# Latent-attention scores from split operands, and one decay product per head, in a four-layer block on one Trainium2 core

## The reference, cut to what matters

```
qn_l, qr_l = queries(cq_l, seq)
q_l = jnp.concatenate([qn_l, apply_rope(qr_l, cos, sin)], axis=-1)
...
s = jnp.einsum('bqhd,bkhd->bhqk', q, k).astype(F32) * ((C_NOPE + C_ROPE) ** -0.5)
p = jax.nn.softmax(s, axis=-1)
```

```
s = jnp.einsum('bhqd,bhkd->bhqk', qc, kh).astype(jnp.float32) * scale
s = s + (cq[..., :, None] - csum[:, :, None, :])
s = jnp.where(kpos[None, :] <= qpos[:, None], s, -jnp.inf)
```

## Time and profile before

| | |
|---|---|
| time, median of 3 runs | 1072.35 us (1072.02 to 1072.69) |
| the profiled execution | 1071.89 us |
| its span, first to last instruction | 1069.9 us |
| PE busy | 1049.8 us (98%) |
| DVE busy | 733.3 us (69%) |
| ACT busy | 591.8 us (55%) |
| chain that ended last | PE 89%, DVE 7%, ACT 2% |
| DMA | 165.41 MB, mean 155 GB/s |

### The profile page before, as it was taken

How to read it: one execution, slowest core, us unless ns; L and a number is a source line. 1 busy time by engine, 2 the same in 40 slices (tenths; PEclk the granted TensorE clock), 3 DMA queues, 4 the chain that set the end, 5 groups by cost and what they waited for, 6 DMA issues and landing times.

```text
span 1069.9 us, 18034 instructions
## 1 busy us (share of the span) xinstructions
PE 1049.8 (98%) x6797; PEld 884.3 (83%) x6797; DVE 733.3 (69%) x1577; ACT 591.8 (55%) x1209; POOL 2.6 (0%) x10
## 2 busy tenths in 40 slices
PE   5999999999999999999999999999999999999997
PEld 3677776788997779989898988889988898888886
DVE  4635567665588756787778766658788778765665
ACT  4534245543364446568776764445567677665444
POOL 0000000000000000000000000000000000000000
PEclk9999999999999999999999999999999999999999
DMA  9998551222342224564555566666464545555662
GB/s 326 336 311 245 181 184 41 60 60 75 83 135 55 78 78 126 140 175 138 138 141 155 145 170 182 193 196 177 129 171 139 139 139 157 157 162 177 194 213 83
DMA packets 203551, 165.41 MB, mean 155 GB/s; under 512 B 7101, under 2 KB 172713, under 8 KB 203465
## 3 DMA queue, kind: packets, MB, share of 16 engines
q1 hardware_dynamic: 202944, 163.28, 52.0%
q0 software_dynamic: 192, 0.66, 0.2%
q10 hardware_dynamic: 328, 0.32, 0.1%
HBM read 163.18 MB, written 1.05 MB: 153 GB/s over the span
## 4 chain that ended last, share of the span: by engine, by line
PE 89%; DVE 7%; ACT 2%; issue 1%; DMA 1%; SPq 0%; ACTq 0%; DVEq 0%
PE pj L2059 23%; PE pj L2061 22%; PE pj L2060 22%; DVE w_lo L1328 2%; PE pj L2153 2%; PE tr L2611 1%; PE ac L2415 1%; PE ac L2550 1%; PE sc L2259 1%; PE tr L2266 1%; PE sc L2401 1%; ACT w_hi L835 1%; PE ac L2280 1%; PE sc L2532 1%; PE sc L2530 1%
## 5 line engine op out<-in xcount | busy, mean ns | idle before, releaser
L1328 DVE TENSOR_TENSOR w_lo<-raw,w_hi 128x1024 fp32r<-128x1024 f32 (+2 forms) x258 | 309.4, 1202 | 148.7 <-ACT w_hi L835 147.8
L835 ACT ACTIVATE w_hi<-raw 128x1024 fp32r<-128x1024 f32 (+2 forms) x258 | 268.0, 1040 | 89.3 <-PE pj L2061 87.3
L2059 PE MATMUL pj<-h_hi,w_hi 128*128 128x256 f32 (+1 forms) x960 | 299.0, 311 | 0.2
L2061 PE MATMUL pj<-h_hi,w_lo 128*128 128x256 f32 (+1 forms) x960 | 291.1, 303 | 0.0
L2060 PE MATMUL pj<-h_lo,w_hi 128*128 128x256 f32 (+1 forms) x960 | 291.0, 303 | 0.0
L2059 PEld LDWEIGHTS pj<-h_hi,w_hi 128*128 128x128 f32 x960 | 183.7, 191 | 19.1 <-issue 10.4
L2061 PEld LDWEIGHTS pj<-h_hi,w_lo 128*128 128x128 f32 x960 | 183.8, 191 | 7.4
L2060 PEld LDWEIGHTS pj<-h_lo,w_hi 128*128 128x128 f32 x960 | 184.0, 192 | 6.2
L2059 PE MATMUL pj<-w_hi,h_hi 128*128 128x512 f32 x344 | 137.4, 399 | 0.4 <-DVE h_lo L1402 0.4
L2061 PE MATMUL pj<-w_hi,h_lo 128*128 128x512 f32 x344 | 134.2, 390 | 0.0
L2060 PE MATMUL pj<-w_lo,h_hi 128*128 128x512 f32 x344 | 134.2, 390 | 0.0
(11 more groups left out here) (358 smaller groups left out, 1473.4 us busy)
## 6 DMA issues: line engine op xcount, KB each, us to landing
raw<-in_w_in_dram SPq DMA_DIRECT2D x152, 512.0 KB, 3.7
ada_raw<-in_ada_w_dram SPq DMA_DIRECT2D x48, 512.0 KB, 7.9
raw<-in_even_w_in_dram SPq DMA_DIRECT2D x28, 512.0 KB, 5.0
raw<-in_w_branch_dram SPq DMA_DIRECT2D x24, 512.0 KB, 3.7
raw<-in_w_out_dram SPq DMA_DIRECT2D x16, 512.0 KB, 3.7
raw<-in_odd_w_in_dram SPq DMA_DIRECT2D x11, 512.0 KB, 3.9
raw<-in_even_w_out_dram SPq DMA_DIRECT2D x8, 512.0 KB, 3.7
raw<-in_odd_w_out_dram SPq DMA_DIRECT2D x8, 512.0 KB, 3.8
```

The costliest lines, as they stand in the source:

```text
L835: last = nc.scalar.activation(hi, src, ACT.Copy)
L1328: last = nc.vector.tensor_tensor(lo, src, hi.bitcast(F32), ALU.subtract)
L2059: nc.tensor.matmul(dst, lh, rh, start=first, stop=False)
L2061: return nc.tensor.matmul(dst, ll, rh, start=False, stop=final)
```

## The change

Four things change.

1. The unrotated scores of the latent attention are made from split operands. `qn` and `kn` are written as a rounded copy by ACT (`qn_hi`, `kn_hi`) and a rest by DVE (`qn_lo`, `kn_lo`), the two in that order on the same bank, and DVE frees it. One `F32` product for a head and a query tile becomes three `F32R` products. The values `vm` are read out by ACT instead of DVE.
2. The decay rows are stored in three blocks of 128 columns, so that one product of 384 columns per head replaces two of 128 and 256.
3. At the start, `condition_turn(0)` and `condition(1)` stand before `spread(0, 4)`, `condition_turn(1)` before `turn_x(4)`, and ACT copies the third set of sums before `modulated_hi(0, 1)`.
4. The last norm takes one step of another form: a reciprocal, one combined operation, a reciprocal, in place of a reciprocal and three operations.

```
-        keys = [("kn", 4 * i + j, "dve" if 4 * i + j in DVE_KEYS else "act") for j in range(4)]
-        return keys + [("vm", (i, t), "dve") for t in range(4)]
+        return [("kn", 4 * i + j, "dve") for j in range(4)] + [("vm", (i, t), "act") for t in range(4)]
     if name == "wq":
-        return [("qn", 2 * i, "act"), ("qn", 2 * i + 1, "act"), ("qr", i, "act")]
+        return [("qn", 2 * i, "dve"), ("qn", 2 * i + 1, "dve"), ("qr", i, "act")]
...
-        decays = [h_hi[:, 0, EARLY[lay]] for lay in range(LAYERS_2)]
+        decays = [h_hi[:, 0:3, EARLY[lay].start:EARLY[lay].start + P] for lay in range(LAYERS_2)]
...
@@ ACT, l1_evacuate
                     elif kind == "kn":
-                        nc.scalar.activation(kn_o[:, i, :], src, ACT.Copy).then_inc(freed["act"], 1)
+                        nc.scalar.activation(kn_hi[:, i, :], src, ACT.Copy).then_inc(nope_hi, 1)
+                    elif kind == "vm":
+                        half, n = i
+                        nc.scalar.activation(v_o[:, n, 512 * half:512 * half + 512], src, ACT.Copy).then_inc(freed["act"], 1)
                     elif kind == "qn":
-                        nc.scalar.activation(qn_o[:, i, :], src[:, 0:SEQ], ACT.Copy, scale=MLA_SCALE).then_inc(freed["act"], 1)
+                        nc.scalar.activation(qn_hi[:, i, :], src[:, 0:SEQ], ACT.Copy, scale=MLA_SCALE).then_inc(nope_hi, 1)
...
@@ DVE, l1_evacuate
-                    elif kind == "vm":
-                        half, n = i
-                        proj_ready(dve, g, None)
-                        nc.vector.tensor_scalar(v_o[:, n, 512 * half:512 * half + 512], bank(g), 1.0, None, ALU.mult)\
+                    elif kind == "qn":
+                        dve.wait_ge(nope_hi, NOPE_ORDER.index((kind, i)) + 1)
+                        nc.vector.scalar_tensor_tensor(qn_lo[i], bank(g)[:, 0:SEQ], MLA_SCALE, qn_hi[:, i, :].bitcast(F32),
+                                                       ALU.mult, ALU.subtract).then_inc(freed["dve"], 1)
+                    elif kind == "kn":
+                        dve.wait_ge(nope_hi, NOPE_ORDER.index((kind, i)) + 1)
+                        nc.vector.tensor_tensor(kn_lo[i], bank(g).rearrange("p (a n) -> p a n", a=2),
+                                                kn_hi[:, i, :].bitcast(F32).rearrange("p (a n) -> p a n", a=2), ALU.subtract)\
                             .then_inc(freed["dve"], 1)
...
-                if s == WKV_SLOT[1]:
-                    for i in DVE_KEYS:
-                        keys_evacuate(i)
...
@@ DVE, the last norm
-                after(nc.vector.reciprocal(y, root))
-                newton(y, term, v).then_inc(last_set, 1)
+                after(nc.vector.reciprocal(term, root))
+                after(nc.vector.scalar_tensor_tensor(term, term, v, root, ALU.mult, ALU.add))
+                nc.vector.reciprocal(y, term).then_inc(last_set, 1)
...
@@ PE, the start
-            spread(0, 4)
             condition_turn(0)
             condition(1)
+            spread(0, 4)
+            condition_turn(1)
             turn_x(4)
-            condition_turn(1)
...
@@ PE, l1_scores
-                    nc.tensor.matmul(sc[:, e, :], qn_o[:, 2 * hp + e, q], kn_o[:, 2 * hp + e, :], start=True, stop=False)
+                    h = 2 * hp + e
+                    nc.tensor.matmul(sc[:, e, :], qn_hi[:, h, q], kn_hi[:, h, :], start=True, stop=False)
+                    nc.tensor.matmul(sc[:, e, :], qn_lo[h][:, q], kn_hi[:, h, :], start=False, stop=False)
+                    nc.tensor.matmul(sc[:, e, :].rearrange("p (a n) -> p a n", a=2), qn_hi[:, h, q], kn_lo[h], start=False,
+                                     stop=False)
...
@@ PE, pair_scores
-                            nc.tensor.matmul(sc[:, e, 0:128], one, decay[0:N_DECAY, 0:P], start=False, stop=False)
-                            last = nc.tensor.matmul(sc[:, e, 128:384], one, decay[0:N_DECAY, :], start=False, stop=True)
+                            last = nc.tensor.matmul(sc[:, e, 0:384].rearrange("p (b n) -> p b n", b=3), one,
+                                                    decay[0:N_DECAY, :, :], start=False, stop=True)
```

More of the change, by code:

```diff
@@ L210 @@
 LAST_OF_CHUNK2 = {c: g for g, (_, _, _, c) in enumerate(G2)}
+NOPE_ORDER = [(k, i) for k, i, _, _ in G1 if k in ("qn", "kn")]
 LAST_GROUP = [LAST_OF_CHUNK1.get(c, -1) for c in range(CB)]
@@ L432, in build_program @@
         w_hi, w_lo = sb("w_hi", [P, NSPLIT, WEL], F32R), sb("w_lo", [P, NSPLIT, WEL], F32R)
+        with nc.sbuf_tensor("parts_o", [P, 7680], F32R) as parts_o:
+            pass
         work = sb("work", [P, 12288])
@@ L478, in build_program @@
         kr_o = work[:, 0:512]
-        qn_o = work[:, 512:2560].rearrange("p (h n) -> p h n", h=C_HEADS)
+        qn_hi = parts_o[:, 512:2560].rearrange("p (h n) -> p h n", h=C_HEADS)
+        qn_lo = [w[:, 3072 + SEQ * h:3072 + SEQ * h + SEQ] for w in (m_hi, m_lo) for h in range(C_HEADS // 2)]
         qr_o = work[:, 2560:3584].rearrange("p (h n) -> p h n", h=4)
-        kn_o = work[:, 3584:7680].rearrange("p (h n) -> p h n", h=C_HEADS)
+        kn_hi = parts_o[:, 3584:7680].rearrange("p (h n) -> p h n", h=C_HEADS)
+        kn_lo = [w[:, 2 * h:2 * h + 2, CTX] for w in (h_hi, h_lo) for h in range(C_HEADS // 2)]
         v_o = work[:, 7680:11776].rearrange("p (n c) -> p n c", n=4)
@@ L579, in build_program @@
         recip_set = sem("recip_set")
+        nope_hi = sem("nope_hi")
         og_set, g_hi_set, g_lo_set = sem("og_set"), sem("g_hi_set"), sem("g_lo_set")
@@ L914, in _ @@
             x_turned_to(6)
+            ada_evacuate(2)
             modulated_hi(0, 1)
@@ L917, in _ @@
             for pair in range(1, 4):
-                ada_evacuate(2 * pair)
+                if pair > 1:
+                    ada_evacuate(2 * pair)
                 ada_evacuate(2 * pair + 1)
@@ L1075, in l1_evacuate @@
                     src = bank(g)
-                    if kind == "vm" or (kind == "kn" and engine == "dve"):
-                        continue
                     proj_ready(act, g, None)
@@ L1979, in _ @@
                         dve.wait_ge(tr_free, TB + lay * NT2 + TR2_OF[("cf", 0)] + 1)
[L1980 to L1985, removed]
-                                                decay[96:N_DECAY, :].bitcast(F32), ALU.subtract).then_inc(decay_set, 1)
+                        decay = decays[lay][:, 1:3, :]
+                        rest = decay_rest.rearrange("p (a n) -> p a n", a=2)
+                        after(nc.vector.tensor_scalar(decay[0:N_DECAY], rest[0:N_DECAY], 1.0, None, ALU.mult))
+                        after(nc.vector.tensor_tensor(rest[64:N_DECAY], rest[64:N_DECAY], decay[64:N_DECAY].bitcast(F32),
+                                                      ALU.subtract))
+                        after(nc.vector.tensor_scalar(decay[64:N_DECAY], rest[64:N_DECAY], 1.0, None, ALU.mult))
+                        after(nc.vector.tensor_tensor(decay[96:N_DECAY], rest[96:N_DECAY], decay[96:N_DECAY].bitcast(F32),
+                                                      ALU.subtract))
+                        nc.vector.tensor_scalar(decays[lay][0:N_DECAY, 0, :], decay[0:N_DECAY, 0, :].bitcast(F32), 1.0, None,
+                                                ALU.mult).then_inc(decay_set, 1)
                     if s == MISC_SLOT and lay + 1 < LAYERS_2:
@@ L2020, in last_gained @@
                 dve.wait_ge(y_sq, n + 1)
-                part = nc.vector.tensor_scalar(col[:, 1, 2 + n:3 + n], y_squares[:, n:n + 1], 1.0 / D, NORM_EPS, ALU.mult, ALU.add)
+                part = nc.vector.tensor_scalar(col[:, 1, 2 + n:3 + n], y_squares[:, n:n + 1], 0.25 / D, 0.25 * NORM_EPS, ALU.mult,
+                                               ALU.add)
                 after(part)
```

7 lines of the change are left out of this document (1 added, 6 removed).

## The result

| | before | changed |
|---|---|---|
| median | 1072.18 us (4 runs, 1071.45 to 1072.69) | 1077.76 us (4 runs, 1075.5 to 1078.54) |
| ratio, 95% interval | | 1.0054 (1.0039 to 1.007) |
| profiled execution | 1071.89 us | 1075.5 us |
| its span | 1069.9 us | 1073.6 us |
| mean granted clock, profiled execution | 0.997 | 0.996 |

The change made the kernel slower by 5.6 us. The profiled execution is the quickest of the four, only 3.6 above that of before, and its mean granted clock is higher than that of the other three.

The account below looks back on a forecast made before the run. PE, busy 98% of the span, was taken as the bound. Scores 3.6 us lost, less 1.5 decay, 0.2 start, 0.2 norm: 1.7 more, 1074.1; clock +0.8 −1.7 gave 1073.2, range 1069.0 to 1076.2.

Parts of the forecast that it names:

- A stall of 2.5 us: Before the first key group of wkv 0, PE waits for DVE's qn reading; pair 0's scores 3.3 us late together.
- The fourth key group of `wkv 1`: PE's group at wkv 1 waits for DVE's first key reading: 3.2 us late, pair 1's 0.42 gain used up.
- one new fall of the clock partly hidden, the old one gone: Likeliest case: stalls, a new half-clock stretch at +0.8 us, the one near 438 us saved at −1.7; 1073.2, chance 0.36.
- The third case: Stalls, old clock fall stays, a new one at wkv 1's fourth key group: 1074.9, or 1075.8 if unhidden; chance 0.30.
- The rule of the Trainium skill: For PE's two new waits: half clock after each, up to 3.4 us more in sum, by the advice against idle gaps.
- The products of the scores: Latent attention on PE: six F32R products cost 1.38 instead of 1.80 us, gaining 0.42 a pair, 3.4 over eight.
- The decay products: Decay product on PE: two of 384 columns take 0.34 instead of 0.56 us; 0.9 to 1.8 gained, 1.5 taken.
- The start: Start of the kernel: PE's 0.8 us wait for ACT goes, but later sums are tied to transfers; 0.2 gained.
- The norm: Last norm, at the chain's end: one DVE step fewer, 0.2 us gained.
- The fourth case: DVE reaches the banks sooner, no stalls: 1067.1, or 1070.8 if only the first goes; chance 0.20 for both.

Follow-up runs that it names:

- filled: Changed kernel plus 11 and 15 idle PE products ahead of the first key group of wkv 0 and the last of wkv 1; 1073.54 us, ratio 1.0021.
- after_again: The changed kernel run once more, unaltered, for another profiled execution; 1076.97 us, ratio 1.0054.
- keys_early: Changed kernel with new order in slots 10 to 12 alone: wkv 1 keys copied before pair 1's exponentials, read before its scaling; 1071.35 us, ratio 0.9997.
- both_early: Changed kernel with keys_early's order, and queries and keys of wkv 0 read before rotations and weight pieces; 1068.36 us, ratio 0.9968.
- early_act: both_early with ACT's copies of qn 0 and qn 1 moved ahead of the two weight pieces of slot 8; 1068.05 us, ratio 0.9967.
- split_early: Kernel before with the split scores alone, in the DVE and ACT orders of early_act; 1067.89 us, ratio 0.9965.

## Why the prediction was wrong

The forecast was 1073.2 and "same"; the time is 1077.76 and slower.

- **The waits were right.** "A stall of 2.5 us" ahead of the first key group, 3.3 with what follows: the wait is 2.77 and the shift 3.3 (from 0.47 ahead to 2.85 behind). The fourth key group of `wkv 1` was put 3.2 late with pair 1's gain used up in it, and on that account it is 3.2 late: 5.72 in all (356.62 less 350.90), of which 2.51 were there behind pair 0's scores. The 3.5 of the sum above counts pair 1's 0.34 apart. Both come through the mechanism stated, DVE's reading queued behind its own weight pieces, and the two orders that put it ahead of them remove the waits.
- **The step that failed is the clock.** It read: "one new fall of the clock partly hidden, the old one gone", +0.8 and −1.7, so the clock was to give 0.9 us back. In its place the traces show one fall (1.2 us) or three (3.2 us) around the waits, and the old fall still there in both; `filled` puts the clock's share of the median at 3.3 us. The forecast was off by 4.2 us there, nearly the whole miss of 4.6. The smaller terms below add about 1.0, which makes 0.6 more than the miss, within the spread of the four runs. It assumed two things at once that nothing in the rows held up: that one fall is all that two new waits bring, though both are longer than every other wait of PE but the one ahead of its first product, and that a fall in a place that the change leaves alone will go.
- **The third case named this mechanism**, "the old fall stays, and a new one comes", 1074.9 to 1075.8 with 0.30. The profiled execution, 1075.5, is in it, though the case was reckoned for a median, and on the scale of the profiled execution, 0.46 lower, it ends at 1075.3. The other executions are beyond it, and its upper end allowed for one fall only. With the three falls that `after_again` shows, at 1.1 each, and the old one kept, the sum would have been 1074.1 + 3.3 = 1077.4.
- **The rule of the Trainium skill**, "TensorE: Matmul & The Clock Gate", section "Why this matters for your kernels", says that idle gaps of PE let the clock fall back. It agrees with `after_again` (about 1.1 us for each fall) and with `filled`, where the same gaps held idle products and the clock stayed at 1.00. It was cited and not weighed enough. But it doesn't say that every gap brings a fall, as the prediction read it, and here not every one does: the wait of 2.8 us was followed by none in the first trace and in `keys_early`, and the 9.1 us ahead of PE's first product by none in any trace (1.00 from 10 to 60 us). The fall at 438 us stands behind no idle gap of this size at all.
- **The products of the scores**: 0.42 a pair was put, 0.34 measured, worth 0.6 to 0.7 us over eight pairs. The 0.23 was read rightly. The 1.80 of before was not: 0.09 of it belong to the step to the 64 rows of the rotated part (340.77 to 341.29 above), which the change keeps, so the six products cost 1.46 and not 1.38 up to that part.
- **The decay products**: 1.5 put, 0.9 measured, the lower end of the bounds: two take 0.44 to 0.46 in the eight places, not 0.34.
- **The start**: 0.2 put, 0.47 between the two traces; tied to the transfer at 67 us as said, with less of a tie. One pair of traces doesn't settle it: `wq 0` begins at 330.29 to 331.91 in four traces with the old start and at 329.67 to 331.89 in eight with the new one, 0.65 apart on average. **The norm**: 0.2 put, 0.1 measured, since the combined operation takes 0.25 to the next start where a plain step took 0.19.
- **The fourth case**, that DVE would be in time, is out: it needs the order of `both_early`.

What stays open: why the fall at 438 us is absent in the traces of `keys_early`, `both_early`, `early_act` and `split_early` and present in the other eight, though the instructions there are the same, and whether the changed kernel could lose it. Those four have the new order at `wkv 1` in common, 75 us earlier, but one trace of each doesn't show that it is the reason: three of the five runs of `both_early` had a mean clock of 0.997 where the traced one had 0.999. The fall stands behind single-column products wherever it was seen, and a similar place at 217 us had it once.

## What to carry to other kernels

When PE is the bound, a product made cheaper is worth its difference only if every bank is still read out in time; a read-out that now takes two engines in turn must be put ahead of work that nobody waits for (weight pieces due two slots later, rotations), and then the same edit goes from 5.6 us lost to 3.8 gained, 1.5 of which are a fall of the clock elsewhere that stayed away. A new wait of PE of 2.8 or 3.6 us can cost more than its length: count a fall of the clock of about 1.1 us for each, perhaps two, and don't count on an old fall to go. If executions of one program lie 2 us apart, compare their mean granted clocks and the time up to the place of the change, and profile it a second time before explaining the median by one trace.

## What the runs showed of the hardware

- A fall of the granted clock to 0.50 can follow a wait of 2.8 us in one execution (335.50) and not in the next (the first trace), and a wait of 3.6 us was followed by one fall or by two. The four runs of `after_again` lie between 1075.4 and 1078.2 us.
- Products that nobody needs, put in the wait, keep the clock: 32.93 instead of 34.13 or 36.15 for the same stretch.
- The fall at 438 us costs 1.5: from the first product behind the single-column ones to the turning of the next operand (`tr`, 16 by 16) it is 4.49 to 4.54 us in the eight traces that have it, and 3.04 or 3.05 in the four that don't.
- The product ahead of a product with 64 rows takes 0.09 more to the next start than its like: 0.52 instead of 0.43 for a record of an `F32` product, 0.32 instead of 0.23 for `F32R`. Ahead of an `F32` product with 128 rows `F32R` takes 0.23 (339.26 to 339.49), so the change of kind is not what costs.
- Two `F32R` products of 384 columns take 0.46 (532.74 to 533.20), where four of 128 and 256 columns took 0.56, so fewer of them saved less than their columns say.
